# Attention values: weights scaled by VectorE before the turn, value products in plain fp32 on alternating column halves

## What is computed

```python
def attend(blk):
    qn, qr = blk
    s = (jnp.einsum('bqhd,bkhd->bhqk', qn, k_nope)
         + jnp.einsum('bqhd,bkd->bhqk', qr, k_rope))
    pr = jax.nn.softmax(s.astype(jnp.float32) * scale, axis=-1).astype(v.dtype)
    return jnp.einsum('bhqk,bkhd->bqhd', pr, v)
```

## Time and profile before

| | |
|---|---|
| median of three runs | 3155.41 us (3155.41 to 3159.03) |
| span of the profiled execution, first to last instruction | 3156.9 us |
| TensorE busy | 3111.0 us, 99% |
| VectorE busy | 2360.7 us, 75% |
| ScalarE busy | 1229.6 us, 39% |
| GpSimd busy | 90.1 us, 3% |
| attention, from the first transposition to the last value product | 1202.41 to 1477.53 us of the span |

### The profile page before, as it was taken

One profiled execution on the slowest core, in us unless ns is written; L12 is line 12 of the kernel. 1 busy time (PEld: TensorE's weight loads), 2 busy tenths in 40 slices (PEclk: granted clock), 3 DMA queues, 4 the chain that ended last, 5 costly groups with the idle time before them and its releaser, 6 DMA issues.

```text
span 3156.9 us, 37986 instructions
## 1 busy us (share of the span) xinstructions
PE 3111.0 (99%) x14840; PEld 2540.0 (80%) x14840; DVE 2360.7 (75%) x4053; ACT 1229.6 (39%) x1920; POOL 90.1 (3%) x113
## 2 busy tenths in 40 slices
PE   8999999999999999999999999999999999999998
PEld 7887888876988888888878888888777788788887
DVE  6777766778869578777598766767797789779636
ACT  4233323335242456655243233222366523423414
POOL 0000000000000002232000000000000000000000
PEclk9999999999999999999999999999999999999999
DMA  3222212113333350003211111111212221122242
GB/s 130 74 74 80 74 60 74 67 61 128 113 91 138 137 187 24 14 28 134 94 54 63 45 54 61 47 54 47 71 56 75 85 78 65 47 71 100 79 168 74
DMA packets 89249, 250.68 MB, mean 79 GB/s; under 512 B 8560, under 2 KB 24304, under 8 KB 87536
## 3 DMA queue, kind: packets, MB, share of 16 engines
q1 hardware_dynamic: 89072, 248.25, 22.7%
HBM read 204.18 MB, written 44.04 MB: 79 GB/s over the span
## 4 chain that ended last, share of the span: by engine, by line
PE 91%; DVE 5%; ACT 2%; issue 1%; DMA 0%; POOL 0%; DVEq 0%; SPq 0%; POOLq 0%; ACTq 0%
PE PS L570 89%; PE PS L575 2%; DVE X L2243 1%; DVE XS L2243 1%; DVE WS L2235 1%; DVE HELD L2297 1%; DVE X L2235 1%; ACT XS L1352 0%; DVE XSf L2235 0%; ACT XSf L1352 0%; DVE TMP L2235 0%; DVE HELD L2235 0%; DVE TMP L2243 0%; DMA RAW<-in_W 0%; ACT TMP L1352 0%
## 5 line engine op out<-in xcount | busy, mean ns | idle before, releaser
L570 PE MATMUL PS<-XS,WS 128*128 128x512 f32 (+1 forms) x6480 | 1514.2, 391 | 18.8 <-DVE XS L2235 8.7
L570 PEld LDWEIGHTS PS<-XS,WS 128*128 128x128 f32 x6480 | 1208.0, 188 | 293.6 <-issue 28.0
L570 PE MATMUL PS<-HS,WS 128*128 128x512 f32 x2208 | 512.5, 391 | 3.1 <-DVE TMP L2235 2.6
L570 PEld LDWEIGHTS PS<-HS,WS 128*128 128x128 f32 x2208 | 415.3, 188 | 93.5 <-DVE TMP L2235 3.5
L2235 DVE TENSOR_TENSOR WS<-RAW,WS 128x512 fp32r<-128x512 f32 (+1 forms) x398 | 347.0, 880 | 176.6 <-ACT WS L1352 176.0
L1352 ACT ACTIVATE WS<-RAW 128x512 fp32r<-128x512 f32 (+1 forms) x398 | 307.6, 779 | 405.1 <-PE PS L570 354.7
L2235 DVE TENSOR_TENSOR X<-PS,X 128x512 f32<-128x512 f32 x272 | 184.1, 688 | 101.8 <-PE PS L570 101.8
L2235 DVE TENSOR_TENSOR TMP<-TMP,PS 128x512 f32<-128x512 f32 x304 | 203.5, 682 | 61.3 <-PE PS L570 58.4
L570 PE MATMUL PS<-T,WS 128*128 128x512 f32 x960 | 230.6, 389 | 0.0
L570 PEld LDWEIGHTS PS<-T,WS 128*128 128x128 f32 x960 | 180.2, 188 | 37.4
L1352 ACT ACTIVATE TMP<-PS 128x512 f32<-128x512 f32 x144 | 85.0, 595 | 301.3 <-PE PS L570 297.6
(11 more groups left out here) (337 smaller groups left out, 3663.5 us busy)
## 6 DMA issues: line engine op xcount, KB each, us to landing
RAW<-in_W SPq DMA_DIRECT2D x263, 512.0 KB, 3.3
RAWX<-in_W SPq DMA_DIRECT2D x30, 512.0 KB, 3.3
DC<-TMP SPq DMA_DIRECT2D x32, 256.0 KB, 2.1
X<-in_xT SPq DMA_DIRECT2D x8, 512.0 KB, 8.8
DX<-X SPq DMA_DIRECT2D x2, 2048.0 KB, 8.7
DCZ<-CA SPq DMA_DIRECT2D x8, 512.0 KB, 4.3
DGA<-TMP SPq DMA_DIRECT2D x16, 256.0 KB, 2.3
DGB<-TMP SPq DMA_DIRECT2D x16, 256.0 KB, 3.1
```

The costliest lines, as they stand in the source:

```text
L570: done = d.matmul(out, l, r, start=first, stop=last)
```

## The change

The exponentials of a block are multiplied by the reciprocals of their row sums before they are turned (in `normal`, a tensor_scalar of 128x1024 in place in PROB). `turn(n)` waits for this (`ve("pn", n)`) instead of the exponentials, and `normal(n-2)` stands first in VectorE's iteration. PT and VH hold plain fp32, with no high and low part. ScalarE copies group 0 of the turned weights, VectorE group 1. `values(j)` is 8 plain fp32 matmuls with 64 stationary columns by 256, which write partitions 0 to 63 of the bank for even n and 64 to 127 for odd n. `row_sums`, `scale_ident` and the final multiplication in `o_out` are gone. VH holds all eight heads, so `heads_v(1, i)` stands in the iterations n = 29 to 32, one in each, and its copies are divided between ScalarE (i = 0, 2) and VectorE (i = 1, 3), as those of heads 0 to 3 are.

```diff
-    VH = at("VH", 128, [128, 8, 4, 2, 64], F32R)
+    VH = at("VH", 128, [128, 8, 8, 64], F32)
-    PT = at("PT", 160, [128, 2, 2, 8, 256], F32R)
+    PT = at("PT", 160, [128, 2, 8, 256], F32)
@@ tensor
             def turn(n):
                 for g in range(2):
-                    e.wait_ge(ac("ex", n), dma("const")("cols"))
-                    e.wait_ge(ve("pt", n - 1, g) if n else ve("vh", 0, 2 + g))
+                    e.wait_ge(ve("pn", n), dma("const")("cols"))
+                    e.wait_ge(turned_out(n - 1, g) if n else values_out(0, 2 + g))
...
-            def row_sums(j):
...
             def values(j):
...
-                for n in range(8):
-                    v = VH[:, n, hd % 4]
-                    both = (out, v.rearrange("p a d -> p (a d)"), PT[:, p, 0, n, :], n == 0, n == 7)
-                    rest = (out[0:64], v[:, 0], PT[:, p, 1, n, :], False, False)
-                    items += [rest, both] if n == 7 else [both, rest]
+                mms([(out[64 * (n % 2):64 * (n % 2) + 64], VH[:, n, hd, :], PT[:, p, n, :], n < 2, n > 5)
+                     for n in range(8)]).then_inc(*mm.inc(*use))
...
-                if n in (34, 35):
-                    for q in ((0,), (1, 2, 3))[n - 34]:
-                        heads_v(1, q)
-                if n >= 3 and n % 2 == 1 and n < 66 and n != 35:
-                    row_sums((n - 3) // 2)
+                if 29 <= n < 33:
+                    heads_v(1, n - 29)
@@ scalar
             def turn_out(n):
-                for g in range(2):
-                    e.wait_ge(mm("tr", n, g))
...
+                act(PT[:, p, 0:4, o:o + 128], PS[:, 6, :].rearrange("p (k q) -> p k q", q=128), ACT.Copy).then_inc(
+                    *ac.inc("pt", n, 0))
@@ vector
             def o_out(j):
-                tt(x, x, ps[64:128, 0:256], ALU.add).then_inc(*ve.inc("ot0", j))
-                e.wait_ge(ve("ot0", j))
-                tt(x, x, ps[0:64, 256:512], ALU.mult).then_inc(*ve.inc("ot", j))
+                tt(x, x, PS[64:128, misc.slot.get(("val", j), 0), 0:256], ALU.add).then_inc(*ve.inc("ot", j))
             def normal(n):
                 e.wait_ge(ac("ex", n))
                 d.reciprocal(ri, sm).then_inc(*ve.inc("ri", n))
+                e.wait_ge(ve("ri", n))
+                ts(PROB[n % 3], PROB[n % 3], ri, None, ALU.mult).then_inc(*ve.inc("pn", n))
             def turn_out(n):
-                for g in range(2):
-                    e.wait_ge(ac("pt", n, g))
-                    low(PT[:, p, 1, 4 * g:4 * g + 4, o:o + 128], PS[:, 6 + g, :].rearrange("p (k q) -> p k q", q=128),
-                        PT[:, p, 0, 4 * g:4 * g + 4, o:o + 128]).then_inc(*ve.inc("pt", n, g))
+                e.wait_ge(mm("tr", n, 1))
...
+                d.tensor_copy(PT[:, p, 4:8, o:o + 128], PS[:, 7, :].rearrange("p (k q) -> p k q", q=128)).then_inc(
+                    *ve.inc("pt", n, 1))
             for n in range(67):
+                if 2 <= n < 66:
+                    normal(n - 2)
                 if 1 <= n < 65:
                     row_max(n - 1)
                 if n >= 5 and n % 2 == 1:
                     o_out((n - 5) // 2)
                 if 2 <= n < 66:
-                    normal(n - 2)
                     turn_out(n - 2)
@@ gpsimd
-        def scale_ident(n):
-            e.wait_ge(ve("ri", n), dma("const")("cols"), *([mm("val", n // 2 - 2)] if n > 3 else []))
-            d.tensor_scalar(weight(n), ident[:], stat(n)[3], None, op0=ALU.mult).then_inc(*po.inc("wt", n))
```

More of the change, by code:

```diff
@@ L517, in values_bank, with values_rows, values_out, turned_out @@
         return PS[:, misc.slot.get(("hv", b, i), 0) if b else 4 + i, :]
+    def values_rows(b, i):
+        return VH[:, 2 * i:2 * i + 2, 4 * b:4 * b + 4, :], values_bank(b, i).rearrange("p (n h d) -> p n h d", n=2, h=4)
+    def values_out(b, i):
+        return ve("vh", b, i) if i % 2 else ac("vh", b, i)
+    def turned_out(n, g):
+        return ve("pt", n, 1) if g else ac("pt", n, 0)
     def hs_free(name, f):
@@ L1010, in heads_v @@
                 if b:
-                    misc.take(use, (ve, "vh", b, i))
+                    misc.take(use, (ve if i % 2 else ac, "vh", b, i))
                     e.wait_ge(*misc.free(use))
@@ L1037, in turn @@
                 for g in range(2):
-                    e.wait_ge(ac("ex", n), dma("const")("cols"))
-                    e.wait_ge(ve("pt", n - 1, g) if n else ve("vh", 0, 2 + g))
+                    e.wait_ge(ve("pn", n), dma("const")("cols"))
+                    e.wait_ge(turned_out(n - 1, g) if n else values_out(0, 2 + g))
                     trs([(PS[:, 6 + g, 128 * k:128 * k + 128], PROB[n % 3][:, g, 128 * k:128 * k + 128], ident[:])
                          for k in range(4)]).then_inc(*mm.inc("tr", n, g))
-            def row_sums(j):
[L1044 to L1048, removed]
             def values(j):
                 hd, p, use = j // 4, j % 2, ("val", j)
-                out, items = PS[:, misc.slot.get(use, 0), 0:256], []
-                for n in range(8):
-                    v = VH[:, n, hd % 4]
-                    both = (out, v.rearrange("p a d -> p (a d)"), PT[:, p, 0, n, :], n == 0, n == 7)
-                    rest = (out[0:64], v[:, 0], PT[:, p, 1, n, :], False, False)
-                    items += [rest, both] if n == 7 else [both, rest]
-                e.wait_ge(ac("pt", 2 * j + 1, 1), ve("pt", 2 * j + 1, 1), ve("vh", hd // 4, 3))
-                mms(items).then_inc(*mm.inc(*use))
+                out = PS[:, misc.take(use, (ve, "ot", j)), 0:256]
+                e.wait_ge(turned_out(2 * j + 1, 0), turned_out(2 * j + 1, 1), values_out(hd // 4, 2), values_out(hd // 4, 3),
+                          *misc.free(use))
+                mms([(out[64 * (n % 2):64 * (n % 2) + 64], VH[:, n, hd, :], PT[:, p, n, :], n < 2, n > 5)
+                     for n in range(8)]).then_inc(*mm.inc(*use))
             for h in range(2):
@@ L1093, in attention @@
                     banks.ends[2 + 2 * (n % 2) + g] = ((ac, "ex", n),)
-                banks.ends[6 + g] = ((ac, "pt", 63, g), (ve, "pt", 63, g))
+                banks.ends[6 + g] = ((ve if g else ac, "pt", 63, g),)
             banks.at += (2 - banks.at) % 8
@@ L1819, in turn_out @@
                 p, j, o = (n // 2) % 2, n // 2, 128 * (n % 2)
-                for g in range(2):
-                    e.wait_ge(mm("tr", n, g))
[L1822 to L1827, removed]
+                e.wait_ge(mm("tr", n, 0))
+                if j > 1:
+                    e.wait_ge(mm("val", j - 2))
+                else:
+                    e.wait_ge(ac("cq", 2), ve("cq", 2), ve("kr", 1, 1))
+                act(PT[:, p, 0:4, o:o + 128], PS[:, 6, :].rearrange("p (k q) -> p k q", q=128), ACT.Copy).then_inc(
+                    *ac.inc("pt", n, 0))
             def exps(n):
@@ L1871, in attention @@
                         k_out(hd + 1, i - 3)
-                if n in (35, 36):
-                    for q in range(2):
-                        v_out(1, 2 * (n - 35) + q)
+                if 30 <= n < 34:
+                    v_out(1, n - 30)
                 if n == 65:
@@ L3029, in v_out @@
             def v_out(b, i):
[L3030 to L3032 removed]
+                if i % 2:
+                    e.wait_ge(mm("hv", b, i), mm("yb", 7, 1))
+                    d.tensor_copy(*values_rows(b, i)).then_inc(*ve.inc("vh", b, i))
                 if b and i == 3:
```

20 lines of the change are left out of this document (9 added, 11 removed).

## The result

The changed kernel takes **3168.9 us** (median of 5 runs, 3166.53 to 3169.08), the kernel before, beside it on the same chip, 3156.38 (3155.41 to 3159.03). The ratio is 1.0036, 95% interval 1.0025 to 1.0047: slower by about 0.4%. The profiled span is 3167.2 us against 3156.9, so +10.3 where the sum of the prediction had +2.8. By the medians the change costs 12.5 us; the traces can't show the other 2.2, since the profiled execution of the kernel before was not a median one: in the other runs the time is 1.8 to 1.9 above the span, which puts it near 3158.8 (later medians of that kernel lie at 3157.46 to 3158.83).

A forecast was written before the change was run, and what follows sets the result against it. TensorE, busy 99%, was taken as the bound; its freed work mostly becomes waits for the scaling. Head losses, V's -6.1, start and slower turns sum to +2.8 us, 3159.7 as span, so 3158; range 3143 to 3174.

The forecast's parts named there:

- A: Rival on value products: column halves don't overlap, 3.55 us instead of 1.90, +53 us, 3211, chance 0.07; milder 3166, 0.08.
- B: Rival on TensorE's clock: waits before turns drop it to 1.2 GHz; one fall per light pair gives 3175; chance 0.09.
- C: Rival on VectorE's scaling: it takes 1.2 us, the second ring takes over at 8.04 a pair, +13, 3171; chance 0.05.
- Values: TensorE's value products per pair: 1.90 us in plain fp32 with overlapping halves, against 1.87 before, so +0.03.
- The ring with TensorE: Loop of turn, scores, values, ScalarE copy, exponentials, reciprocal, scaling, next turn: 7.56 us for two blocks, TensorE idle 1.1.
- The second ring: Loop between VectorE and ScalarE: scaling, maximum, negative maximum, exponentials, reciprocal; 3.57 us a block, 7.14 a pair, just fits.
- light pairs: Pairs of blocks in which nothing is made for the next head: from 7.13 to 7.56 us, +0.43 each.
- full pairs: Pairs full of TensorE's work, where TensorE stays the bound: each gains about 0.57 us.
- the pair with K: In heads 1, 3, 5: ScalarE's copies of K delay the next copy and exponentials, the turn waits 2.2 us, +1.6.
- V in heads 3 and 4 together: V products of heads 4 to 7: four take 5.8 us, about 2.6 filling existing waits; net -6.1 us.
- scaling of 128x1024 in SBUF 0.752: VectorE's scaling before the turn, taken from the row with a scalar, SBUF to SBUF; upper bound 1.38, lower 0.69 us.
- turn, scores and values, 0.79 + 1.46 + 1.90 = 4.15 us: TensorE's part of its ring, from an even block's turn until it begins the odd block's turn: 4.15 us.

The follow-up runs named there:

- one_half: The changed kernel with all eight value products of a pair in one column half, the last addition of halves replaced by a stand-in: 3218.57 us, ratio 1.0192.
- order_undone: The changed kernel with the turn one block later and GpSimd paced by the scaling, VectorE again scaling a block before the next one's maximum: 3147.16 us, ratio 0.9965.
- gpsimd_paced: The changed kernel with GpSimd's work of each block waiting until VectorE has scaled that block's weights: 3163.13 us, ratio 1.0019 to the kernel before.
- scaling_by_product: The changed kernel with the scaling written as a product of two tensors instead of a tensor by a scalar: 3179.26 us, ratio 1.0068 to the kernel before.
- scaling_alone: The kernel before plus scaling ahead of the turn, without row sums or scaled identity; weights and V still split, fp32r value products: 3190.04 us, ratio 1.0102.
- v_late: The changed kernel with the four V products back at blocks 34 and 35, each bank still emptied by one engine: 3171.15 us, ratio 1.0043.
- scaling_halves: The changed kernel with each scaling cut into two of 512 columns, the turn's first half waiting only for the first: 3165.19 us, ratio 1.0023.
- turn_later: The changed kernel with turn, copies, value product and adding up one block later, and VectorE's maximum ahead of the previous block's scaling: 3139.96 us, ratio 0.9948.

## Why the prediction was right in direction, and where its size came from

The forecast was 3158 us, in effect no change, with 3143 to 3174 as the range. 3168.9 lies in the range, but above the 3150 to 3166 that had more than half of the chances, and none of A, B and C, whose prices of 3166 to 3175 are the nearest to it, came true. The mechanism, a ring that turns TensorE's freed work into waits for the scaling, was right, and the forecast of about no change was not: the change costs 10 to 12 us. That the range held it is owed to the width that the rivals gave it.

Right, by its steps:
- Values: 1.90 taken, 1.88 measured, and one_half shows that the overlap of halves is the reason. Of the two estimates the state products' 1.90 was right; the estimate of 2.15 by the Trainium skill ("TensorE: Matmul & The Clock Gate", packing of small matmuls) was too high here.
- The ring with TensorE: every hand-over as predicted. The second ring: 7.14 predicted, 7.09 where it can be seen by itself (two light pairs of order_undone).
- Scaling 0.75 undisturbed, VectorE's copy out of PSUM 0.69, full pairs -0.57 (measured -0.48 to -0.58), the pair with K +1.6 (+1.54), V in heads 3 and 4 together (-4.65 predicted with their pairs; -3.9 in gpsimd_paced).
- Rival B did not come in light pairs: waits of 0.9 to 1.6 before a turn left TensorE at 2.4 GHz (granted 1.00), and so B's 3175 did not come. The estimate by the Trainium skill ("TensorE: Matmul & The Clock Gate", PE-mode transpose) was not this case. A fall was priced at 1.5 at least and costs 1.57; two came in the changed kernel, after waits of 2.83. The kernel before had one at the end of attention, which is gone.

What was wrong is the size, +10.3 instead of +2.8, in two terms:
1. **"scaling of 128x1024 in SBUF 0.752"** as the price of every scaling. The row that I took it from had nothing of GpSimd beside it. Four pairs lost 6.6 us to two scalings that wait out a subtraction of GpSimd: 3.8 by themselves, 2.8 by the fall of the clock behind each. The prediction wrote "GpSimd its 64 products with the identity; neither ends a wait any more, so both are worth nothing". They are worth nothing as work, but they waited for each reciprocal and so paced GpSimd's queue. Without them its five weight splits start as soon as their input is there, some beside a scaling (the first begins at 1245.81 and not 1258.92, right behind the work on Q). gpsimd_paced gives 5.8 us of the total back with one wait. The Trainium skill ("GPSIMD Engine Reference", Specifications) had the rule, as told at scaling_by_product, and I did not apply it.
2. **"turn, scores and values, 0.79 + 1.46 + 1.90 = 4.15 us"**. It is 4.30. A turn at 0.85 I had counted apart; the 0.10 for entering the 64-column form stood in the text for the unfavourable case only and was left out of the sum. In some 20 pairs that is 2.0 us.

6.6 + 2.0 is 8.6; head 7 with the end cost 0.5 instead of 1.3 and the first turn 0.2 instead of 0.3, which leaves the 7.5 to within 0.2. And "ScalarE loses a copy ... worth nothing" holds beside the row sums only; scaling_alone and v_late show that without the single parts of weights and V the scaling would have cost 20 us more, of which the copy in the ring explains a part.

The larger lesson is in what the prediction did not ask: whether the ring has to be there. It saw 21 us of freed work turned into waits, and one block of lag plus an exchange of two instructions' order gives most of it back (-17.5 us against the kernel before, -20 with GpSimd paced).

## What to carry to other kernels

An operation put on the path between two engines costs its place in the ring, not its duration on an engine with slack: add up the ring, and where a third buffer allows it, consume one round later and let the engine first do what the others wait for. When an instruction is removed from a queue, ask what it paced; GpSimd's subtractions beside VectorE's SBUF-to-SBUF scaling held one of them up for most of the other here. Price a form by a row in which it begins as it will begin in the new place.

## What was not expected of the hardware

- VectorE's SBUF-to-SBUF scaling beside GpSimd's subtraction took 2.65 us instead of 0.75; where VectorE's product form came first, GpSimd's took 3.42 instead of 2.35. I had expected the product form to be free of it; it took up to 1.66 for 1.23.
- A wait of 2.0 us before a turn came nine times in the traces of the changed kernel, gpsimd_paced, v_late and one_half. After three of them TensorE's granted clock fell to the lower level (1398.08 in gpsimd_paced, 1255.00 in v_late, 1435.76 in one_half); after six it did not (1254.76 and 1402.33 in the changed kernel, among others). In scaling_halves a wait of 2.64 (ended at 1362.71) brought no fall and one of 2.65 (1436.03) did. The turn behind a wait can still take 1.09 and the fall come with the scores after it, as at 1398.08 and 1436.03, so the granted clock has to be read and not the turn. At the end of attention it fell behind less: in order_undone beside a wait of 1.6 (1458.4), in turn_later without one over 1.5 (0.53 in 1453.4 to 1457). What decides stays open; no run was made for it. Since a fall costs 1.57 us, totals of single kernels here differ by this much through it, and differences of that size are read from pairs.
- Eight plain fp32 products of 64 columns into one column half take 3.59 us, into alternating halves 1.88.
